# Slot values read along with the gathered rows, an item's second outward chunk after the next item's hidden products, ScalarE's scaled copies after its activation

## What is computed

```python
logits = xf @ w_router + b_router                 # 32 experts
top_val, top_idx = lax.top_k(logits, 4)
comb = ...                                        # softmax weights of the 4 chosen, 0 elsewhere
for e in range(32):
    hh = xf @ w_expert_in[e] + b_expert_in[e]     # 1024 x 2048
    gate = min(hh[:, :1024], 7); lin = clip(hh[:, 1024:], -7, 7)
    act = (lin + 1) * gate * sigmoid(1.702 * gate)
    y = y + comb[:, e:e+1] * (act @ w_expert_out[e] + b_expert_out[e])   # 1024 x 1024
```

## Time and profile before

| | us |
|---|---|
| median of 3 runs | 1527.59 (1525.19 to 1530.2) |
| the profiled execution | 1528.83 |
| its span, first to last instruction | 1527.1 |
| TensorE busy | 1270.6 (83% of the span) |
| VectorE, ScalarE, GpSimd busy | 359.4, 299.8, 185.6 |
| mean granted TensorE clock | 0.917 of full |
| moved by DMA | 534.81 MB, mean 350 GB/s |

### The profile page before, as it was taken

One profiled execution on the slowest core, in us unless ns is written; L12 is line 12 of the kernel. 1 busy time (PEld: TensorE's weight loads), 2 busy tenths in 40 slices (PEclk: granted clock), 3 DMA queues, 4 the chain that ended last, 5 costly groups with the idle time before them and its releaser, 6 DMA issues.

```text
span 1527.1 us, 27763 instructions
## 1 busy us (share of the span) xinstructions
PE 1270.6 (83%) x11003; PEld 701.5 (46%) x11004; DVE 359.4 (24%) x779; ACT 299.8 (20%) x622; POOL 185.6 (12%) x307
## 2 busy tenths in 40 slices
PE   6999999999999789999964599586969666964596
PEld 3777887776887434444421144232423222321143
DVE  1023113333631423222211122111322112211123
ACT  3000122442100222222211122121212111211111
POOL 0240100110180011111100001000100000000010
PEclk9999999999999899999978799897989878887698
DMA  9876724999546388699999999999999999999994
GB/s 368 304 285 227 269 109 150 387 398 394 182 160 248 129 348 325 261 419 416 419 426 424 427 419 422 424 422 427 420 422 413 428 420 418 410 428 425 425 411 198
DMA packets 77023, 534.81 MB, mean 350 GB/s; under 512 B 6602, under 2 KB 7778, under 8 KB 50129
## 3 DMA queue, kind: packets, MB, share of 16 engines
q1 hardware_dynamic: 67026, 502.39, 80.4%
q0 software_dynamic: 9568, 30.96, 6.1%
q10 hardware_dynamic: 391, 0.93, 0.2%
HBM read 509.03 MB, written 27.69 MB: 351 GB/s over the span
## 4 chain that ended last, share of the span: by engine, by line
PE 56%; DMA 40%; DVE 1%; SPq 1%; issue 1%; ACT 0%; POOL 0%; DVEq 0%; POOLq 0%; ACTq 0%
DMA ring<-in_w_expert_in_dram 22%; PE ps L770 16%; PE ps L950 12%; DMA moe_ring<-in_w_expert_out_dram 10%; PE ps L972 9%; DMA moe_ring<-in_w_expert_in_dram 3%; PE ps L527 2%; PE ps L919 2%; PE ps L812 2%; PE ps L853 2%; PE ps L819 2%; PE ps L799 2%; DMA ring<-in_state_ret_dram 1%; DMA sample_rows<-moe_rows 1%; DMA ring<-in_w_ada_dram 1%; PE ps L574 1%
## 5 line engine op out<-in xcount | busy, mean ns | idle before, releaser
L950 PE MATMUL ps<-ring,xgT 128*32 128x512 f32 x2352 | 320.9, 668 | 173.4 <-DMA ring<-in_w_expert_in_dram 172.8
L770 PE MATMUL ps<-hT,ring 128*128 128x264 f32 x1152 | 267.3, 390 | 2.1 <-DMA ring<-in_w_in_dram 2.1
L770 PEld LDWEIGHTS ps<-hT,ring 128*128 128x128 f32 x1152 | 218.2, 191 | 55.1 <-issue 15.5
L950 PEld LDWEIGHTS ps<-ring,xgT 128*32 128x32 f32 x2352 | 66.3, 116 | 313.3 <-DMA ring<-in_w_expert_in_dram 180.8
L972 PE MATMUL ps<-moe_ring,actT 128*32 128x256 f32 x3136 | 181.8, 381 | 4.2 <-DMA moe_ring<-in_w_expert_out_dram 3.9
L1584 DVE TENSOR_TENSOR xg<-ps,sh_q 128x256 f32<-128x256 f32 x48 | 20.4, 425 | 546.1 <-PE ps L919 546.1
L1217 ACT ACTIVATE ostage<-ps,slots_w 32x256 f32<-32x256 f32 x184 | 85.8, 466 | 273.8 <-PE ps L972 272.0
L972 PEld LDWEIGHTS ps<-moe_ring,actT 128*32 128x32 f32 x3136 | 99.7, 111 | 86.2 <-issue 18.2
L950 PE MATMUL ps<-moe_ring,xgT 128*32 128x512 f32 x784 | 95.5, 605 | 27.3 <-DMA moe_ring<-in_w_expert_in_dram 27.3
L919 PE MATMUL ps<-rows,picked 128*32 128x256 f32 (+1 forms) x1176 | 80.2, 387 | 1.3 <-DVE picked L1536 1.3
L1209 ACT COPY actT<-ps 128x256 f32<-128x256 f32 x49 | 18.2, 372 | 310.6 <-PE ps L527 310.6
(11 more groups left out here) (310 smaller groups left out, 1164.8 us busy)
## 6 DMA issues: line engine op xcount, KB each, us to landing
ring<-in_w_expert_in_dram SPq DMA_DIRECT2D x96, 2048.0 KB, 12.4
moe_ring<-in_w_expert_out_dram SPq DMA_DIRECT2D x64, 2048.0 KB, 12.4
moe_ring<-in_w_expert_in_dram SPq DMA_DIRECT2D x32, 2048.0 KB
ring<-in_w_in_dram SPq DMA_DIRECT2D x18, 2048.0 KB, 12.0
ring<-in_w_ada_dram SPq DMA_DIRECT2D x12, 2048.0 KB, 8.1
ring<-in_state_ret_dram SPq DMA_DIRECT2D x8, 1024.0 KB, 11.0
vslot<-in_state_ret_dram SPq DMA_DIRECT2D x8, 1024.0 KB, 11.5
out_dram<-ring POOLq DMA_DIRECT2D x8, 1024.0 KB, 8.8
```

What stands on the lines that cost most here:

```text
L770: mm = nc.tensor.matmul(ps[:, j, 0:T], ring[s][:, k, j * P:(j + 1) * P], hT[:, k, :], start=(k == 0), stop=(k == KC - 1))
L950: mm = nc.tensor.matmul(side(0, g), xgT[:, a, j * SLOTS:(j + 1) * SLOTS], w[:, a, g * COL:(g + 1) * COL], start=False, stop=(j == 3 and a ...
```

## The change

Three edits in the expert stage, and what goes with them.

1. `rows` gets two more columns for each of its four column blocks, and VectorE copies the two `slot_v` columns of the expert into them for every item (`values_ready`). The gather then moves 258 columns in place of 256, and its last two give number and weight of the slots. `pick` is gone, but for the first item (`first_slots`). `take_slots` on VectorE comes right behind the taking of the gathered rows.
2. The second half of the outward product of item q-1 (chunk 5) is put at the end of item q, behind `hidden(2)`, `hidden(3)` and `turn_gathered`. The first half (chunk 4) stays. Items behind the loop (`kept`) keep both halves where they were.
3. ScalarE runs `squash(q)` ahead of `take_outward(q - 1)`.

```diff
             def gather(q, first=False):
                 pe.wait_ge(picked_ready, 3 * q + 3)
+                if not first:
+                    pe.wait_ge(values_ready, q)
+                    pe.wait_ge(slots_taken, SLOT_STEPS * q)
+                cols = QUARTER if first else QUARTER + 2
...
-                        mm = nc.tensor.matmul(side(1, g)[:, 0:QUARTER], picked[0:n, t, 0:SLOTS], rows[0:n, t, g * QUARTER:(g + 1) * QUARTER],
+                        mm = nc.tensor.matmul(side(1, g)[:, 0:cols], picked[0:n, t, 0:SLOTS], rows[0:n, t, g, 0:cols],
...
-            def outward(q, e):
-                pe.wait_ge(out_bias_ready, q + 1)
-                pe.wait_ge(eo_taken, q + 1)
-                for g in range(SIDES):
-                    nc.tensor.matmul(side(2, g)[:, 0:QUARTER], bias_out[:], bsplit_out[:, g * QUARTER:(g + 1) * QUARTER], start=True, stop=False)
-                pe.wait_ge(act_taken, q + 1)
-                for h in range(2):
+            def outward(q, e, halves=(0, 1)):
+                if 0 in halves:
+                    outward_begun(q)
+                for h in halves:
...
                 biases(q)
                 pe.wait_ge(xgT_ready, q + 1)
                 hidden(0, e)
                 turn_hidden(q - 1)
                 hidden(1, e)
-                outward(q - 1, before)
+                outward(q - 1, before, (0, 1) if kept else (0,))
                 gather(q + 1)
                 hidden(2, e)
                 hidden(3, e)
                 if kept:
                     combine(0)
                 turn_gathered(q + 1)
-                pe.wait_ge(slots_taken, SLOT_STEPS * q + SLOT_STEPS)
-                pick(q + 1, after)
+                if not kept:
+                    outward(q - 1, before, (1,))
...
             with act_e.Fori(1, prev) as q:
                 take_hidden(q - 1)
+                squash(q)
                 take_outward(q - 1)
-                squash(q)
...
             def choose(q, e):
                 for t in range(3):
                     ts(picked[:, t, :], ...).then_inc(picked_ready, 1)
+                cp(rows[:, :, :, QUARTER:QUARTER + 2], slot_v[:, :, bass.ds(e, 1), :].broadcast_to([P, 3, SIDES, 2])).then_inc(values_ready, 1)
...
             def take_gathered(q):
                 dve.wait_ge(xg_ready, q + 1)
                 tt(xg[:], ps[:, 1, 0:QUARTER], sh_q[:], ALU.add).then_inc(xg_taken, 1)
+                take_slots(bass.ds(q, 1))
...
             with dve.Fori(0, prev) as q:
                 after = dve.value_load(item_i[0:1, bass.ds(q + 1, 1)], min_val=0, max_val=E - 1)
-                dve.wait_ge(slots_ready, q + 1)
+                dve.wait_ge(xg_ready, q + 1)
                 choose(q + 1, after)
                 take_gathered(q + 1)
                 make_act(q)
-                take_slots(q + 1, bass.ds(q + 1, 1))
```

More of the change, by code:

```diff
@@ L230, in trunk_kernel @@
         rows_at = top[0] = v_at
-        rows = new("rows", [P, 3, D])
+        rows = new("rows", [P, 3, SIDES, QUARTER + 2])
         assert top[0] <= v_at + 12544
@@ L918, in gather, with first_slots @@
                     for g in range(SIDES):
-                        mm = nc.tensor.matmul(side(1, g)[:, 0:QUARTER], picked[0:n, t, 0:SLOTS], rows[0:n, t, g * QUARTER:(g + 1) * QUARTER],
+                        mm = nc.tensor.matmul(side(1, g)[:, 0:cols], picked[0:n, t, 0:SLOTS], rows[0:n, t, g, 0:cols],
                                               start=(t == 0), stop=(t == 2))
                 mm.then_inc(xg_ready, 1)
-            def pick(q, e):
-                pe.wait_ge(picked_ready, 3 * q + 3)
+            def first_slots():
                 for t in range(3):
-                    values = slot_v[:, t, 0, :] if e is None else slot_v[:, t, bass.ds(e, 1), :].rearrange("p a b -> p (a b)")
-                    mm = nc.tensor.matmul(ps[:, 1, QUARTER:QUARTER + 2], picked[:, t, :], values, start=(t == 0), stop=(t == 2))
+                    mm = nc.tensor.matmul(ps[:, 1, QUARTER:QUARTER + 2], picked[:, t, :], slot_v[:, t, 0, :], start=(t == 0), stop=(t == 2))
                 mm.then_inc(slots_ready, 1)
@@ L974, in outward, with outward_begun @@
                     mm.then_inc(chunk_used[4 + h], 1)
+            def outward_begun(q):
+                pe.wait_ge(out_bias_ready, q + 1)
+                pe.wait_ge(eo_taken, q + 1)
+                for g in range(SIDES):
+                    nc.tensor.matmul(side(2, g)[:, 0:QUARTER], bias_out[:], bsplit_out[:, g * QUARTER:(g + 1) * QUARTER], start=True, stop=False)
+                pe.wait_ge(act_taken, q + 1)
             gather(0, True)
@@ L984, in _ @@
             pe.wait_ge(routes_ready, 1)
-            pick(0, None)
+            first_slots()
             hidden(2, 0)
             prev = pe.value_load(last_i[0:1, 0:1], min_val=E - 2, max_val=ITEMS - 2)
-            second = pe.value_load(item_i[0:1, 1:2], min_val=0, max_val=E - 1)
-            pe.wait_ge(slots_taken, SLOT_STEPS)
-            pick(1, second)
             gather(1)
@@ L1187, in _ @@
                 for h in range(2):
-                    nc.scalar.activation(rows[:, t, h * COL:(h + 1) * COL], ps[:, 2 * t + h, :], ACT.Copy, scale=rstd3[:, t:t + 1]).then_inc(rows_ready, 1)
+                    nc.scalar.activation(rows[:, t, 2 * h:2 * h + 2, 0:QUARTER], ps[:, 2 * t + h, :].rearrange("p (g n) -> p g n", g=2), ACT.Copy, scale=rstd3[:, t:t + 1]).then_inc(rows_ready, 1)
             act_e.wait_ge(exp_in, 1)
@@ L1538, in _ @@
                 cols = slice(h * COL, (h + 1) * COL)
-                stt(rows[0:TS, 2, cols], ps[0:TS, (7, 4)[h], :], rstd3[0:TS, 2:3], sh_sample[:, cols], ALU.mult, ALU.add).then_inc(last_rows_ready, 1)
+                stt(rows[0:TS, 2, 2 * h:2 * h + 2, 0:QUARTER], ps[0:TS, (7, 4)[h], :].rearrange("p (g n) -> p g n", g=2), rstd3[0:TS, 2:3],
+                    sh_sample[:, cols].rearrange("p (g n) -> p g n", g=2), ALU.mult, ALU.add).then_inc(last_rows_ready, 1)
             dve.wait_ge(counted, 1)
@@ L1597, in make_act @@
                 tt(act[:], glu_l[:], glu_s[:], ALU.mult).then_inc(act_ready, 1)
-            take_slots(0, slice(0, 1))
+            dve.wait_ge(slots_ready, 1)
+            take_slots(slice(0, 1))
             with dve.Fori(0, prev) as q:
                 after = dve.value_load(item_i[0:1, bass.ds(q + 1, 1)], min_val=0, max_val=E - 1)
-                dve.wait_ge(slots_ready, q + 1)
+                dve.wait_ge(xg_ready, q + 1)
                 choose(q + 1, after)
```

8 lines of the change are left out of this document (3 added, 5 removed).

## The result

The changed kernel took 1612.51 us (median of 4 runs, 1608.74 to 1618.67) against 1528.87 us before (4 runs, 1525.19 to 1530.2): ratio 1.0554, 95% interval 1.0534 to 1.0574. The forecast of 1600 us was 12.5 us low, within its range of 1540 to 1655. The profiled execution of the changed kernel is the longest of its runs (1618.67, span 1616.9), 89.8 us in its span above the profiled one of before.

What follows compares the result with a forecast made beforehand. The prediction took the expert stage to be bound by loads, TensorE counting only where their queue runs dry. Standstill +75.6 us and `pick` -3.7 gave +72, on a median of 1527.59: 1600 us, range 1540 to 1655.

Steps and rivals of the forecast that it cites:

- The mechanism: Loads' queue: chunk 5's buffer, freed only behind hidden(3), delays its load, so DMA engines run empty; 2.7 us per expert.
- The way from landing to issue: From chunk 3's landing through hidden(3) and half an outward product to chunk 5's issue: 4.16 us.
- The standstill: DMA engines empty around chunk 5's late issue: 2.7 us per expert, 28 experts, 75.6 us.
- The first term: Idle start of chunk 5's load: 7.6 us against 4.9 in a full queue, less 0.7 beside chunk 4: 2.0 us per expert.
- The 0.7 us for the slowest engine: After a standstill each expert waits anew for the slowest of 16 DMA engines: 0.7 us more, between 0 and 1.4.
- A: Rival: TensorE's clock also falls at hidden(3) after a longer wait; 28 x 1.4 = 39 us on top, 1640 us; chance 0.2.
- -3.7 us for `pick`: Six matmuls of `pick` gone saves 0.73 us in five items around experts 1 and 2, where TensorE is the bound.
- ScalarE's order, 0: Four copies behind the sigmoid end before the PSUM bank is needed; the later scatter has room: 0 us, program end as before.
- The other terms at 0: VectorE's copy of the values, the gather's new waits and its 2 extra columns cost nothing.
- B: Rival: short standstill, chunk 4 hides the slow start; 0.3 to 1.0 us lost per expert, 1532 to 1552 us; chance 0.2.
- C: Rival: the loads' queue never runs dry, leaving only the 3.7 us gain: 1523.9 us; chance 0.05.
- D: Rival: TensorE's wait stays, new gather waits eat `pick`'s saving, queue stays full: 1527.6 us; chance 0.05.

Runs made afterwards that it cites:

- the filler: The changed kernel with six matmuls of zeros put between hidden(2) and hidden(3), where TensorE waits for chunk 3: 1598.97 us (4 runs).

## Why the prediction was right

**The mechanism: right.** The loss is the move's: 1611.16 us with the move and `pick` kept, 1533.3 without it, and 1532.83 with the product in two pieces but the second ahead of the wait for chunk 3. It hangs on the time from landing to issue: 3.42 us instead of 4.28 makes the turn shorter (31.12 us for 32.21). And it is the queue's lead that counts: 29.85 us again where one more load lay ahead.

**The way from landing to issue: right,** 4.28 us for 4.16.

**The standstill, 2.0 + 0.7 = 2.7 us an expert: a little large.** The first term is right, the second was at fault. Where the way was 4.28, a one-item turn took 32.21 us for 29.85, 2.36 more. Two-item turns without a fall of the clock (in the kernel with the filler, 692.30 to 724.87) took 32.6 for a mean of 30.4 before, 2.15 more. Over the whole stretch it is 2.13 to 2.27, or 60 to 64 us for 75.6. The 0.7 us for the slowest engine, which I took between 0 and 1.4, does not show: the rates from 820 to 824 us account for the whole 2.4 us of the turn beside them, and the first term alone gives 2.1, 1.2 and 7.1 us where 2.13 to 2.27, 1.24 and 7.13 were measured. The picture behind the first term was not quite so: chunk 5 is not issued 0.7 us before the engines are done but about half a microsecond after, and what made up for it is that the 7.6 us were taken whole, from issue to landing. By the figures of the Trainium skill, "DMA: Bandwidth & Descriptors", section on the fixed cost of a transfer, which the page gives for loads issued by GpSimd, the forecast had worked out an estimate of 1.2 us an expert; the turns measure nearly twice that, and they decide.

**The clock, left out of the sum: wrong.** The forecast set a chance of 0.2 on A and 0 us in its sum. Over the 28 turns the way from landing to issue was 5.22 us in the mean, 0.94 more than 4.28, which is 26 us; by the filler it is 24. A came true at 0.9 us an expert and not at 1.4, because only 14 of these 28 waits made the clock fall. After 1.0 us of idle time no `hidden(3)` was slow, after 3.95 it was the earlier trace rows, and the waits of the changed kernel, 0.7 to 4.1 us, fill the gap between: of 7 waits of 2.7 us 3 were followed by a slow `hidden(3)` (the one at 848.65, 1.92 us, was not), and above 3.2 us nearly all (as at 1080.88, 3.64 us). "TensorE: Matmul & The Clock Gate" of the Trainium skill, section "Loop structure matters more than you think", tells of cold matmuls between waits of 8 us; in this case waits of 3.2 to 4.1 us were enough in 13 of 14 cases.

**-3.7 us for `pick`: wrong.** It gave nothing: an item without any wait for loads takes 14.31 us for 14.30. Its matmuls lay beside a wait, that of the next biases for the readers of the hidden PSUM bank, which the row of `pick` did not show since it was covered.

**ScalarE's order, 0: wrong by about 5 us.** 0 holds inside the loop (DMA share 1.00), not at the end, where the last scatter comes 7.7 us later and the reading back 2.7. "The end of the program is as before" was the step that failed.

**The other terms at 0: right.** The values in the gather and VectorE's copy cost nothing (1528.36 for 1528.99).

**The sum.** By the profiled spans: 85.8 us in the 28 turns (26 for the clock by the ways; the 60 left are put down to the standstill, for which the filler's trace has 62 by itself), 0.3 before them, and from `hidden(3)` of expert 31 to the end 34.3 us for 30.5, 3.7 more: 89.8, as measured. The forecast of +72 was near since its errors stand against each other in part: 16 too much for the standstill, 26 left out for the clock, and `pick` and the end, 3.7 us each, on the side of the clock. That it came within 12.5 us of the median owes something to luck. DMA share 0.93 (forecast 0.92), 382 GB/s (390), one-item turns 32.2 us (32 to 33). **B**, the short standstill, is out (over 2.1 us an expert, not 0.3 to 1.0), as are **C**, the queue that never runs dry, and **D**, the change that does nothing.

**Open.** Why of two waits of 2.7 us one makes the clock fall and the other does not. The length of the wait is not all: with both halves at the end 8 of 9 waits of 1.8 to 2.5 us were followed by a slow `hidden(3)`, and with half of chunk 5's product left out 1 of 10 of 2.7 us.

## What to carry to other kernels

When loads are the bound, ask of every buffer how much is still queued at the moment its next load is issued: that is its slack. If its last use stands behind a wait for a load near the end of the same queue, the slack is what is queued behind that load less the way back, and once it is gone the loss comes again in every turn. Such a use belongs ahead of the wait, or the buffer's load later in the queue. And matmuls that look like pure cost may stand where the engine would wait anyway; look at what comes next before counting them as a gain.

## What the hardware showed unasked

Engines that run empty are slow to start again. Chunk 5 issued 0.6 us before the last queued load would land (4.9 - 4.28) lost 2.1 to 2.4 us, issued 1.5 us before it still 1.2 to 1.3; with 5.8 us of lead nothing was lost. A small positive lead by landings is none for the engines: they were out of work about half a microsecond before the issue, and in the microseconds around it the rate went 66, 229, 82, 295 and only then 442 GB/s. And TensorE's clock, 2.4 GHz before the wait, stood at 1.2 GHz for the matmuls behind 13 of 14 pauses of 3.2 to 4.1 us, 3 of 7 of 2.7 us, and none of 10 shorter ones in the changed kernel; where a small loss of the loads makes such pauses, it is paid for twice.
